# Splitting projections between small products, masking sooner, and forming bonus sums early in a hybrid decoder step

## The chip, the cores and the metric

The kernel runs on one core of a Trainium2 chip, as one launch of one program. The time is the device time of that launch in microseconds (us); less is better.

## The reference

One inference step of one layer, for 256 new prompt rows and 8 sample sequences of 8 rows (320 rows of 1024 together, all float32).

```
h = rmsnorm(x); proj = h @ w_in                       # 3840 columns
# HGRN2 group (4 heads of 128): chunked gated linear recurrence with states
# RWKV-7 group (8 heads of 64): r, k, v and low-rank decay, a, g from proj, mixed with the row before
kk = k * k_k / |k * k_k|;  k = k * (1 + (a - 1) * k_a)
S_t = S * w + (S . -kk) (kk * a)^T + v k^T;  y = S_t . r       # per token and head, state 64 x 64
bonus = sum_over_a_head(r * k * r_k) * v
y = (groupnorm(y) + bonus) * g
x = x + concat(o_hgrn, y) @ w_out
x = x + moe(rmsnorm(x))                                # top 4 of 32 experts, clamped SwiGLU
return rmsnorm(x), both groups' new states, last normalised rows
```

## The kernel before

Everything is written by hand: each engine has its own list of instructions in the order in which it issues them, and semaphores order the engines against each other. The work around the change is the mixer of the layer, before the experts.

**Projections.** `w_in` is read in 15 chunks of 256 columns into a ring of three slots (`WORDER`, `NSLOT`). SyncE's list loads chunk n when the tiles of chunk n - 3 are done. Each chunk gives two tiles, so there are 30 projections, numbered 0 to 29; `proj_part(n, c0, c1)` issues the matmuls c0 to c1 of the eight 128-row steps of tile n. ScalarE evicts each tile into `raw`, and VectorE mixes it with the row before (`mix_tile`) or gates it (`gate_tile`), in the order of the tile numbers.

**PSUM.** Each product that fills a bank is a unit. `psum_units()` names, in the order of TensorE's list, the units with their bank (the third argument of `add`), and in a second list (`ends`, `end(...)`) the order in which they are completed. `free(stage, i)` on TensorE waits until the unit that had the bank before has been read (`<stage>_ready`); `wait_filled` on a reader waits for the count of completed units. A unit whose bank is another one waits for another reader.

**The RWKV part.** The token-by-token recurrence is solved in chunks of 64 tokens. Gram products of the scaled rows (`gM`, `gN`, `gT`, `gK`, `gRb`, `gRk`; 64-row matmuls, L1126 and L1136) feed a triangular solve by doubling in five steps (`make_z`, `make_w`, `make_t`, L1152 and L1160; `take_z`, `take_w`, `take_t` on VectorE). Between the steps TensorE's list has projections 23 to 29 (L914). `W_` and `T_` start from unit matrices, which GpSimd copies into `hx` (L823) when the scaled rows are ready (`rw_ready`). The hidden states of the HGRN2 group are made by `hstate` (L1014) and added on VectorE (L2623, L2624).

**The sample sequences.** Their states are turned (`s0t`), multiplied with queries (`Rs`, L1254 and L1272), and give `Us` (L1283) and the values `Ys` (L1318 to L1320). `state_update(jj)` (L1214) makes the new HGRN2 states in two halves from itoks masked by sequence (`masked(jj)` on ScalarE, 8 copies); VectorE adds them (`add_states`, L2713). `bks` (L1301) holds the turned, decayed keys of the samples; `btok` and `ktok` (`turn_tokens`, L1313) hold the turned keys of the prompt.

**The bonus.** VectorE makes r * k * r_k into `rbon` (L2603). Late in the part, after the products `UW` and `UX` (L1332), four matmuls with a block matrix of ones sum over each head and spread the sum over its 64 rows (L1339); VectorE multiplies by v (L2781). Then follow `C` (L1351) and the accumulation of the states (L1505, L1508).

**Weights.** `w_out` is loaded in two halves: `wo[1]` into the `spare` slot, after all chunks of `w_in`, and `wo[0]` when projection 27 is done. The expert weights start when the units `Y0` are complete.

## Time and profile before

| | |
|---|---|
| median of 3 runs | 1212.39 us (1211.2 to 1213.39) |
| the profiled execution | 1214.35 us |
| its span (first to last instruction) | 1212.4 us |
| busy share of the span | TensorE 98%, VectorE 36%, ScalarE 21%, GpSimd 4% |
| mean granted TensorE clock | 0.998 of full speed |
| HBM read | 430.01 MB |

The span runs from the first to the last instruction of the program; the execution's time has about 2 us more around it. A start in the profile is counted from the span's start. TensorE's matmuls are pipelined, so a busy share near all of the span doesn't say that it works at its peak. An idle time in brackets behind an instruction is that of its engine just before it, with what ended it; "issue" means that nothing in the profile ended it.

### The profile page before, as it was taken

What the parts mean: (1) busy time and instruction counts of PE and PEld (TensorE: products, weight loads), DVE (VectorE), ACT (ScalarE), POOL (GpSimd) and SP (SyncE); (2) the same over time, 40 slices, a digit from 0 to 9 for tenths busy, and PEclk for the clock granted to TensorE, in tenths of its full rate; (3) what the DMA queues carried; (4) which work ended last, traced back from release to release, by engine and by line L of the source; (5) the groups of instructions that cost most, each with busy time, mean ns of one, the idle gap of its engine ahead of it and who ended that gap; (6) DMA issues with size and microseconds to landing.
All of it is one profiled execution on the core that took longest, in us unless ns stands there. A gap on an engine that the chain in (4) does not pass through costs nothing.

```text
span 1212.4 us, 18239 instructions
## 1 busy us (share of the span) xinstructions
PE 1187.4 (98%) x7814; PEld 572.9 (47%) x7814; DVE 440.9 (36%) x962; ACT 259.5 (21%) x630; POOL 44.7 (4%) x101
## 2 busy tenths in 40 slices
PE   8999999999999999999999999999999999999996
PEld 6777677745344344444443444344444444343332
DVE  3357954753413332332233132313322323232324
ACT  3114435422221111111121212021111111111213
POOL 8000110100000000000000000000000000000000
PEclk9999999999999999999999999999999999999999
DMA  9732302498999999999999999999999999999996
GB/s 285 183 105 71 122 31 72 125 414 334 409 426 429 426 414 428 426 432 431 431 429 431 431 431 432 431 426 431 429 432 432 430 430 431 432 432 428 422 424 231
DMA packets 49387, 436.09 MB, mean 360 GB/s; under 512 B 11525, under 2 KB 26952, under 8 KB 31770
## 3 DMA queue, kind: packets, MB, share of 16 engines
q1 hardware_dynamic: 48180, 431.74, 86.4%
q0 software_dynamic: 960, 3.02, 0.8%
q8 instruction: 63, 1.03, 0.3%
q10 hardware_dynamic: 166, 0.15, 0.0%
q14 instruction: 18, 0.15, 0.0%
HBM read 430.01 MB, written 4.89 MB: 359 GB/s over the span
## 4 chain that ended last, share of the span: by engine, by line
PE 86%; DMA 10%; DVE 2%; issue 1%; SPq 0%; ACT 0%; DVEq 0%
PE bank L1634 33%; PE bank L1670 16%; PE bank L914 9%; PE bank L1600 7%; DMA ring<-in_w_gate_up 5%; PE bank L1704 4%; PE bank L1395 3%; DMA ring<-in_w_down 3%; PE bank L1661 3%; DMA mix<-in_w_gate_up 2%; PE bank L1695 1%; PE bank L1152 1%; PE bank L901 1%; PE bank L947 1%; DMA hx<-in_state_shift 0%
## 5 line engine op out<-in xcount | busy, mean ns | idle before, releaser
L1634 PE MATMUL bank<-ring,mix 128*64 128x512 f32 x1504 | 344.8, 598 | 3.3 <-DMA ring<-in_w_gate_up 3.1
L1634 PEld LDWEIGHTS bank<-ring,mix 128*64 128x64 f32 x1504 | 101.3, 136 | 201.0 <-issue 197.7
L1670 PE MATMUL bank<-ring,mix 128*64 128x512 f32 x736 | 168.2, 598 | 0.8 <-DMA ring<-in_w_down 0.8
L2986 DVE TENSOR_TENSOR hTb<-bank,w2a 128x512 f32<-128x512 f32 x32 | 22.1, 692 | 361.3 <-PE bank L1661 361.3
L914 PE MATMUL bank<-hTb,ring 128*128 128x328 f32 (+1 forms) x416 | 120.6, 444 | 0.0
L2218 ACT ACTIVATE mix<-bank,nf 128x256 f32<-128x256 f32 x64 | 26.8, 470 | 431.3 <-PE bank L1600 431.2
L1634 PE MATMUL bank<-mix 128*64 128x512 f32 x500 | 112.7, 595 | 1.8 <-DMA mix<-in_w_gate_up 1.8
L3046 DVE TENSOR_TENSOR mix<-mix,bank 128x512 f32<-128x512 f32 x70 | 48.2, 688 | 159.5 <-PE bank L1704 143.5
L914 PEld LDWEIGHTS bank<-hTb,ring 128*128 128x128 f32 x416 | 77.8, 192 | 33.8 <-issue 2.0
L1670 PEld LDWEIGHTS bank<-ring,mix 128*64 128x64 f32 x736 | 49.3, 136 | 89.9 <-issue 84.0
L1634 PEld LDWEIGHTS bank<-mix 128*64 128x64 f32 x500 | 35.1, 137 | 71.7 <-issue 70.0
L1600 PE MATMUL bank<-mix,hx 128*128 128x256 f32 x240 | 66.1, 418 | 0.0
L3014 DVE SCALAR_TENSOR_TENSOR y_low<-bank,gc,y_high 64x512 fp32r<-64x512 f32 x62 | 46.5, 750 | 49.6 <-ACT y_high L2293 49.1
L1600 PEld LDWEIGHTS bank<-mix,hx 128*128 128x128 f32 x240 | 55.5, 300 | 9.1 <-issue 8.4
L2293 ACT ACTIVATE y_high<-bank,gc 64x512 fp32r<-64x512 f32 x62 | 42.3, 682 | 74.1 <-DVE gc L3028 38.3
L2273 ACT COPY g2w<-bank 128x512 f32<-128x512 f32 x64 | 34.3, 593 | 99.8 <-PE bank L1634 99.8
L1670 PE MATMUL bank<-mix 128*64 128x512 f32 x240 | 54.8, 598 | 0.0
L1704 PEld LDWEIGHTS bank<-y_high,slot_rows 128*128 128x128 f32 (+1 forms) x96 | 16.2, 186 | 62.5 <-issue 62.5
L1661 PEld LDWEIGHTS bank<-idg,g2w 128*128 128x128 f32 x256 | 33.2, 209 | 26.0 <-issue 26.0
L2283 ACT ACTIVATE bank<-hTb 128x512 f32<-128x512 f32 x32 | 19.2, 602 | 113.9 <-DVE hTb L2988 113.9
L1704 PE MATMUL bank<-y_high,slot_rows 128*128 128x512 f32 (+1 forms) x96 | 42.3, 480 | 0.0
L1661 PE MATMUL bank<-idg,g2w 128*128 128x128 f32 x256 | 39.3, 296 | 0.0
(448 smaller groups left out, 1086.7 us busy)
## 6 DMA issues: line engine op xcount, KB each, us to landing
ring<-in_w_gate_up SPq DMA_DIRECT2D x30, 4096.0 KB, 22.9
ring<-in_w_gate_up SPq DMA_DIRECT2D x33, 2048.0 KB, 14.4
ring<-in_w_down SPq DMA_DIRECT2D x15, 4096.0 KB, 23.7
mix<-in_w_gate_up SPq DMA_DIRECT2D x10, 4096.0 KB, 23.7
ring<-in_w_down SPq DMA_DIRECT2D x14, 2048.0 KB, 13.8
mix<-in_w_gate_up SPq DMA_DIRECT2D x11, 2048.0 KB, 13.2
mix<-in_w_down SPq DMA_DIRECT2D x5, 4096.0 KB, 25.0
ring<-in_w_in SPq DMA_DIRECT2D x14, 1024.0 KB, 5.5
```

The costliest lines, as they stand in the source:

```text
L914: last_ = mm(b_[:, 0:nn], slot(chunk)[:, c, P * k:P * k + P], hT[:, c, 0:nn], start=(c == 0), stop=(c == KT - 1))
L1395: last_ = mm(o_, lhs_, wo[c_ // 4][:, c_ % 4, 512 * h_:512 * h_ + 512], start=(c_ == 0), stop=(c_ == KT - 1))
L1600: last_ = mm(o, rows_of(tile_, c, r), sel[tile_][0:TN[tile_], :], start=(first and tile_ == TORD[0]), stop=(tile_ == TORD[2]), skip_group_ ...
L1634: last_ = mm(b_[64 * half:64 * half + 64, :].rearrange("s (p q) -> s p q", q=4), toks, cols[:, half], start=(c == 0), stop=(c == KT - 1))
L1661: last_ = nc.tensor.transpose(b_[:, P * q:P * q + P], src[:, q:NCOL:4], ident[:, :])
L1670: last_ = mm(b_[r:r + 64, :], lhs, w[:, o:o + NCOL], start=(j == 0 and q == 0), stop=(j == 1 and q == 3))
L1704: last_ = mm(o[:, :], scatr[r[g], g, P * tile_:P * tile_ + P], y_[r[g], g, :], start=(y_ is yhir and g == half), stop=(stop and y_ is ylor ...
L2218: ins = a(xg[n // 4 % 2][:, 256 * c:256 * c + 256], b[:, 256 * x:256 * x + 256], ACT.Copy, scale=nf2[int(n // 4 >= EW // 4)][:, c:c + 1])
L2273: cp(o, b[:, :]).then_inc(S("gu_read"), 1)
L2293: ins = a(yhir[r, k, :], banks[2][r, :], ACT.Copy, scale=gc[r, g:g + 1])
L3014: ins = v.scalar_tensor_tensor(out=ylor[r, k, :], in0=banks[2][r, :], scalar=gc[r, g:g + 1], in1=yhif[r, k, :], op0=ALU.mult, op1=ALU.subt ...
L3046: ins = v.tensor_tensor(o, o, b[:, :], ALU.add)
```

## The change

1. The bonus sums are formed early, in a new unit `bsum` behind `hosa`: four matmuls of 32 columns each put a head sum into rows of one bank, and ScalarE copies it into `rbon[:, 0, :]`. Where the bonus matmuls stood, each of the four tiles now has two matmuls that are 32 rows deep and spread one row of `rbon` over 64 rows. VectorE's bonus products wait for all four.
2. The unit matrices are copied into `hx` by ScalarE, behind the eviction of projection 22, instead of by GpSimd.
3. The load of `wo[1]` moves from behind the last chunk of `w_in` to a place ahead of chunk 6.
4. Projections are divided anew: 25 as 4 + 2 steps, W(1), 2 steps; 28 as 5 steps, W(3), 3 steps; 29 as 4 steps, then Z(4), `Us` and `gRk`, then 4 steps. The completion order and the banks follow.
5. `masked(1)` on ScalarE moves ahead of the copy of `Us`; `bks` moves ahead of `R0` on TensorE and on ScalarE; on VectorE the gating of projection 29 moves behind `gRk`.
6. The `Ys` products come all before the turned keys, and grouped by kind, the two row halves in turn; before, a quarter of them came ahead of each turned tile.

```diff
+    add("bsum", 1, (0,))
     add("hs2", 1, (1,))
     add("proj", 1, (7,))
-    add("gM", 3, (2, 3, 1))
+    add("gM", 3, (2, 3, 0))
     add("gN", 3, (4, 5, 6))
-    add("gT", 2, (7, 0))
-    add("s0t", 4, (5, 6, 7, 0))
-    add("gT", 1, (1,))
+    add("gT", 2, (7, 1))
+    add("s0t", 4, (5, 6, 7, 1))
+    add("gT", 1, (0,))
...
+    add("W", 3, (0, 1, 2))
     end("proj", 25)
-    add("W", 3, (0, 1, 2))
-    add("T", 3, (3, 4, 5))
-    add("gK", 3, (6, 7, 0))
+    add("T", 3, (3, 5, 6))
+    add("gK", 3, (7, 0, 4))
...
-    add("proj", 1, (3,))
+    add("proj", 1, (3,), ended=False)
     add("W", 2, (4, 5))
+    end("proj", 28)
...
-    add("proj", 1, (6,))
+    add("proj", 1, (7,), ended=False)
     add("Z", 2, (4, 5))
     add("Us", 1, (1,))
     add("gRk", 3, (2, 3, 4))
+    end("proj", 29)
     add("atok", 2, (5, 6))
+    add("bks", 1, (1,))
     add("R0", 2, (7, 0))
-    add("bks", 1, (1,))
...
@@ SyncE
+                if n == 6:
+                    load(wo[1], w_out[:, 4:8, :], "x1_wo1_in")
                 if n:
                     load(slot(n), w_in[:, :, 512 * g + 256 * u:512 * g + 256 * u + 256], f"ring{n % NSLOT}")
...
-            load(wo[1], w_out[:, 4:8, :], "x1_wo1_in")
@@ GpSimd
-            pool.wait_ge(S("rw_ready"), 1)
-            g.tensor_copy(hx[:, 0:2 * W5].rearrange("p (x t) -> p x t", t=64), mC[:, 6:7, :].broadcast_to([P, 2 * W5 // 64, 64]))\
-                .then_inc(S("eye_ready"), 1)
@@ TensorE
             filled(last, "hosa")
+            pe.wait_ge(S("rbon_in"), 4)
+            b = free("bsum", 0)
+            for j in range(4):
+                last = mm(b[32 * j:32 * j + 32, 0:NT], blk[:, 0:P:4], rbon[:, j, :], start=True, stop=True)
+            filled(last, "bsum")
             hstate("hs2", 1)
...
             make_z(1)
-            proj_part(25, 4, KT)
+            proj_part(25, 4, 6)
             make_w(1)
+            proj_part(25, 6, KT)
             make_t(1)
...
-            proj_part(28, 0, KT)
+            proj_part(28, 0, 5)
             make_w(3)
+            proj_part(28, 5, KT)
             make_t(3)
...
-            proj_part(29, 0, KT)
+            proj_part(29, 0, 4)
             make_z(4)
...
             gram("gRk", rk, rr)
+            proj_part(29, 4, KT)
             tokens("atok", rkk, 2)
...
             for j in range(4):
                 for p in range(2):
-                    o = b[half(p), half(j)]
-                    mm(o, us[half(p), j, :], Rb_[2][half(p), j, :], start=True, stop=False, skip_group_check=True)
-                    mm(o, vtoks[half(p), j, :], Rk_[2][half(p), j, :], start=False, stop=False, skip_group_check=True)
-                    last = mm(o, yts[half(p), j, :], ident[half(p), half(p)], start=False, stop=True, skip_group_check=True)
-                if j == 3:
-                    filled(last, "Ys")
+                    mm(b[half(p), half(j)], us[half(p), j, :], Rb_[2][half(p), j, :], start=True, stop=False, skip_group_check=True)
+                for p in range(2):
+                    mm(b[half(p), half(j)], vtoks[half(p), j, :], Rk_[2][half(p), j, :], start=False, stop=False, skip_group_check=True)
+                for p in range(2):
+                    last = mm(b[half(p), half(j)], yts[half(p), j, :], ident[half(p), half(p)], start=False, stop=True,
+                              skip_group_check=True)
+            filled(last, "Ys")
+            for j in range(4):
                 turn_tokens(("btok", "ktok")[j // 2], (ra, rk)[j // 2], j % 2)
...
-            pe.wait_ge(S("rbon_in"), 4)
+            pe.wait_ge(S("bonus_ready"), 1)
             for j in range(4):
+                r = slice(32 * j, 32 * j + 32)
                 b = free("bonus", j)
-                filled(mm(b[:, 0:NT], blk[:, :], rbon[:, j, :], start=True, stop=True), "bonus")
+                for p in range(2):
+                    c = 32 * j + 16 * p
+                    last = mm(b[half(p), 0:NT], ident[r, c:c + 1].broadcast_to([32, 64]), rbon[r, 0, :], start=True, stop=True)
+                filled(last, "bonus")
@@ ScalarE
                     a(hsq, htok, ACT.Square).then_inc(S("osq"), 1)
+                    ready(cp(rbon[:, 0, :], wait_filled("bsum", 0)[:, 0:NT]), "bonus")
+                if n == 22:
+                    act.wait_ge(S("rw_ready"), 1)
+                    a(hx[:, 0:2 * W5].rearrange("p (x t) -> p x t", t=64), mC[:, 6:7, :].broadcast_to([P, 2 * W5 // 64, 64]), ACT.Copy)\
+                        .then_inc(S("eye_ready"), 1)
...
                         ready(own_rows(e, rRs, 0), "Rs")
-                if n == 29:
+                    masked(1)
                     ready(cp(us[:, :, :], wait_filled("Us", 0)[:, 0:256].rearrange("p (j v) -> p j v", v=RN)), "Us")
-            masked(1)
...
@@ VectorE
             take_z(4)
-            gate_tile(29)
             dve.wait_ge(S("unit_filled"), U("gRk", 3))
...
             set_masked("gRk", Rk_, 9, 11)
+            gate_tile(29)
...
             dve.wait_ge(S("gpre_ready"), 4)
+            dve.wait_ge(S("unit_filled"), U("bonus", 4))
             for j in range(4):
                 b = wait_filled("bonus", j)
```

## Rows read from the trace of the kernel before

**Rows 1.** The page: its span, instruction packets, and the chain by engine.

```profile
span 1212.4 us, 18239 instructions
...
q8 instruction: 63, 1.03, 0.3%
...
PE 86%; DMA 10%; DVE 2%; issue 1%; SPq 0%; ACT 0%; DVEq 0%
```

**Rows 2.** Waits of SyncE's queue: us in total, times, longest.

```profile
SPq L640 <- PE bank L1540: 47.4, 1, 47.4
```

**Rows 3.** TensorE's timeline, 119 to 227 us: start, duration, instruction, idle before.

```profile
119.85 0.77 PE L1008 MATMUL bank<-hx,g2w 128*32 128x320 f32 x8
...
145.75 0.62 PE L1136 MATMUL bank<-mix 64*64 64x64 f32 x13 [1.68 <-DVE ring L2624]
...
148.96 2.02 PE L1105 MATMUL bank<-idg,ring 128*128 128x128 f32 x16 [0.22 <-DVE hx L2655]
...
153.10 0.99 PE L1152 MATMUL bank<-hx,mix 64*64 64x64 f32 x53 [1.40 <-issue]
...
168.41 1.14 PE L1152 MATMUL bank<-mix,hx 64*64 64x32 f32 x64
...
172.39 1.09 PE L1126 MATMUL bank<-mix 64*64 64x64 f32 x59 [0.85 <-issue]
...
197.46 1.14 PE L1152 MATMUL bank<-mix,hx 64*64 64x32 f32 x64
...
200.90 0.42 PE L1272 MATMUL bank<-ring 64*32 64x64 f32 x23 [1.12 <-issue]
201.25 1.14 PE L1214 MATMUL bank<-ring 32*128 32x512 f32 x8
...
213.13 1.14 PE L1214 MATMUL bank<-ring 32*128 32x512 f32 x8
...
222.79 2.42 PE L1339 MATMUL bank<-mix,g2w 128*128 128x320 f32 x8
...
226.12 0.30 PE L1505 MATMUL bank<-ring,hTb 64*64 64x64 f32 x8
```

**Rows 4.** TensorE between its pauses: length, busy (matmuls), clock, DMA share, GB/s.

```profile
153.09:172.38 19.29, 18.43 (x507) 1.00 0.04 13
172.38:200.89 28.51, 27.39 (x760) 1.00 0.22 77
```

**Rows 5.** GpSimd's timeline at the copy of the unit matrices.

```profile
141.12 2.52 POOL L823 COPY hx<-mC 128x2560 f32<-128x2560 f32 x1 [34.67 <-DVE dc L2617]
```

**Rows 6.** All runs of VectorE's L2481: ns least, median, most; first and last start.

```profile
L2481 DVE TENSOR_TENSOR hx<-raw x14: 174/174/2106, 69.8 to 169.6; 128x8 f32<-128x8 f32 x14
```

**Rows 7.** ScalarE's timeline, its longest operation before the change's place.

```profile
137.97 1.27 ACT L2100 ACTIVATE ring<-mix 128x1280 f32<-128x1280 f32 x1
```

**Rows 8.** DMA issues: count, KB each, us from issue to landing.

```profile
spare_slot<-in_w_out SPq DMA_DIRECT2D x1, 2048.0 KB, 11.7
```

**Rows 9.** VectorE's timeline, 170 to 227 us.

```profile
170.37 0.95 DVE L2689 TENSOR_TENSOR hx<-hx,bank 128x256 f32<-128x256 f32 x3
...
198.83 0.75 DVE L2689 TENSOR_TENSOR hx<-hx,bank 128x256 f32<-128x256 f32 x2
...
202.48 2.48 DVE L2713 TENSOR_TENSOR ring<-ring,bank 128x512 f32<-128x512 f32 x4 [1.52 <-PE bank L1214]
...
214.36 2.48 DVE L2713 TENSOR_TENSOR ring<-ring,bank 128x512 f32<-128x512 f32 x4 [0.78 <-PE bank L1214]
...
222.15 0.69 DVE L2775 COPY ring<-bank 64x512 f32<-64x512 f32 x1 [0.40 <-PE bank L1332]
...
224.90 1.68 DVE L2781 TENSOR_TENSOR mix<-mix,bank 128x320 f32<-128x320 f32 x4
```

**Rows 10.** DMA queues, from 150.6 to 153.1 us and from 194.9 to 197 us.

```profile
q8 instruction: 1, 0.02, 2.3%
...
q8 instruction: 1, 0.02, 3.1%
```

More of the change, by code:

```diff
@@ L174, in psum_units @@
     add("gRk", 3, (2, 3, 4))
+    end("proj", 29)
     add("atok", 2, (5, 6))
+    add("bks", 1, (1,))
     add("R0", 2, (7, 0))
-    add("bks", 1, (1,))
     add("hsend", 4, (2, 3, 4, 5))
     add("W", 2, (6, 7))
-    add("Ys", 1, (0,), ended=False)
+    add("Ys", 1, (0,))
     add("btok", 2, (1, 2))
-    add("ktok", 2, (3, 4), ended=False)
-    end("ktok", 0)
-    end("Ys", 0)
-    end("ktok", 1)
+    add("ktok", 2, (3, 4))
     for x in range(2):
@@ L604, in _ @@
                 params(nm, A[src].rearrange("a (h p) -> (a h) p", p=P))
+            w_out = A["w_out"][0].rearrange("(c p) n -> p c n", p=P)
             for n, (g, u) in enumerate(WORDER):
@@ L632, in _ @@
                              A["norm_ffn"][0].rearrange("(j p r) -> p j r", p=P, r=r), "router_in")
-            w_out = A["w_out"][0].rearrange("(c p) n -> p c n", p=P)
-            load(wo[1], w_out[:, 4:8, :], "x1_wo1_in")
             sync.wait_ge(S("unit_filled"), U("proj", 28))
@@ L863, in free @@
                     s, k, _ = UNITS[BEFORE[n_]]
-                    s, k = {"nmT": ("params", 1), "bc": ("params", 2), "params": ("params", 3), "hT": (("hT", "hTo_lb")[k % 2], k // 2), "S0": ("S", k + 2), "Y0": ("Y", k), "xo": ("xo", k + 1)}.get(s, (s, k))
+                    s, k = {"nmT": ("params", 1), "bc": ("params", 2), "params": ("params", 3), "hT": (("hT", "hTo_lb")[k % 2], k // 2), "S0": ("S", k + 2), "Y0": ("Y", k), "xo": ("xo", k + 1), "bonus": ("bonus", k + 1), "bsum": ("bonus", 0)}.get(s, (s, k))
                     pe.wait_ge(S(f"{s}_ready"), k + 1)
@@ L1285, in _ @@
             gram("gRk", rk, rr)
+            proj_part(29, 4, KT)
             tokens("atok", rkk, 2)
+            pe.wait_ge(S("bk_scaled"), 2)
+            b = free("bks", 0)
+            for s, src in enumerate((ra, rk)):
+                for j in range(4):
+                    for p in range(2):
+                        o = 256 * s + 64 * j
+                        last = mm(b[half(p), o:o + 64], src[half(p), j, NP_:NT], ident[half(p), half(p)], start=True, stop=True)
+            filled(last, "bks")
             b = [free("R0", 0), free("R0", 1)]
@@ L1294, in _ @@
                             filled(last, "R0")
-            pe.wait_ge(S("bk_scaled"), 2)
-            b = free("bks", 0)
-            for s, src in enumerate((ra, rk)):
-                for j in range(4):
-                    for p in range(2):
-                        o = 256 * s + 64 * j
-                        last = mm(b[half(p), o:o + 64], src[half(p), j, NP_:NT], ident[half(p), half(p)], start=True, stop=True)
-            filled(last, "bks")
             state_update(1)
@@ L1316, in _ @@
                 for p in range(2):
-                    o = b[half(p), half(j)]
-                    mm(o, us[half(p), j, :], Rb_[2][half(p), j, :], start=True, stop=False, skip_group_check=True)
-                    mm(o, vtoks[half(p), j, :], Rk_[2][half(p), j, :], start=False, stop=False, skip_group_check=True)
-                    last = mm(o, yts[half(p), j, :], ident[half(p), half(p)], start=False, stop=True, skip_group_check=True)
-                if j == 3:
-                    filled(last, "Ys")
+                    mm(b[half(p), half(j)], us[half(p), j, :], Rb_[2][half(p), j, :], start=True, stop=False, skip_group_check=True)
[5 more added lines that the diff above has]
+            filled(last, "Ys")
+            for j in range(4):
                 turn_tokens(("btok", "ktok")[j // 2], (ra, rk)[j // 2], j % 2)
@@ L1335, in _ @@
                                 filled(last, ("UW", "UX")[p])
-            pe.wait_ge(S("rbon_in"), 4)
+            pe.wait_ge(S("bonus_ready"), 1)
             for j in range(4):
+                r = slice(32 * j, 32 * j + 32)
                 b = free("bonus", j)
-                filled(mm(b[:, 0:NT], blk[:, :], rbon[:, j, :], start=True, stop=True), "bonus")
+                for p in range(2):
+                    c = 32 * j + 16 * p
+                    last = mm(b[half(p), 0:NT], ident[r, c:c + 1].broadcast_to([32, 64]), rbon[r, 0, :], start=True, stop=True)
+                filled(last, "bonus")
             def head(x_, p_):
@@ L2142, in _ @@
                 ready(ins, "atok")
+            ready(cp(bks[:, :, :, :].rearrange("p s j v -> p (s j v)"), wait_filled("bks", 0)[:, :]), "bks")
             for p in range(2):
@@ L2149, in _ @@
                     ready(cp(o, b), "R0")
-            ready(cp(bks[:, :, :, :].rearrange("p s j v -> p (s j v)"), wait_filled("bks", 0)[:, :]), "bks")
             act.wait_ge(S("unit_filled"), U("hsend", 8))
@@ L2925, in _ @@
             sent(1)
-            dve.wait_ge(S("bonus_ready"), 4)
+            dve.wait_ge(S("bonus_ready"), 5)
             for j in range(4):
```

## The prediction

> **What bounds the kernel now.** I read the page first, then TensorE's timeline from 115 to 310 us, where every edit of this change lies, then for each of its pauses the timeline of the engine that it waited for. The page's chain of work gives TensorE 86% and DMA 10% of a span of 1212.4 us [rows 1]. The expert part, from about 236 us on, streams weights; its loads are released by SyncE after one wait of 47.4 us that TensorE's last state values end [rows 2]. So what the earlier part gains or loses up to that point moves the whole rest by as much. Nothing after it is edited but a counter value.
>
> Up to there TensorE is hardly ever idle, and its pauses are of two kinds. Two are named: 1.68 us at 145.75 and 0.22 at 148.96, both for VectorE [rows 3]. The others say "issue": 1.40 at 153.10, 0.85 at 172.39, 1.12 at 200.90 [rows 3]. They are not spread at will. From one to the next lie 507 and 760 matmuls [rows 4], four and six times 126.7. The page lists 63 instruction packets for 1.03 MB [rows 1], about 16 KB each. I read this as TensorE's program arriving in pieces of some 127 matmuls with their weight loads, and a pause where a piece is late. The pauses lie among 64-row products, which use up a piece in about 2 us; a projection of 4.5 us lets the next piece catch up.
>
> The first named pause has its cause on another engine. GpSimd's copy of unit matrices runs from 141.12 for 2.52 us [rows 5]; of the 14 subtractions of 8 columns on VectorE the median is 0.174 us, and one takes 2.106 [rows 6]: the one that meets the copy; both end near 143.65. The hidden-state update that TensorE waits for stands behind it.
>
> **The change, part by part.** All sums are made against the profiled execution (1214.35 us, its span plus 1.9) and carried to the median of the three runs, 1212.39, unchanged.
>
> *A, up to projection 24.* The copy goes to ScalarE. Its price is not in the trace; 1280 elements take ScalarE 1.27 [rows 7], so 2560 take about 2.5 (bounds 2.5 as on GpSimd, twice that for a source read by broadcast; I take the nearest row). It starts when the same vector instruction releases it, so it ends where GpSimd's did, near 143.6. The blocked subtraction falls back to 0.17; the bank of the third Gram part also changes from the hidden state's to the sums', evicted by ScalarE near 139.6. Each alone would end most of the 1.68. The pause of 1.40 falls in a stretch where a 2 MB output-weight load and a prior ring load keep the DMA engines full; that load (11.7 us from issue to landing [rows 8]) moves to about 46 us, ahead on SyncE's queue of projection weights that are needed four projections, some 18 us, later. The bonus sums are added here: the key-norm sums of the same form take 0.77 [rows 3]. So A = -(1.68 + 0.22 + 1.40) + 0.77 = -2.5. Bounds: 0 if the piece that paused at 153.10 is late in another place, -3.0 if pipeline refill after each pause goes too.
>
> *B, projection 25 to the key Gram.* Two of its last four steps now follow the product W(1). The vector engine's list still has the mixing of projection 25 ahead of W's additions. Before, the additions began at 170.37, 1.96 after the projection's end at 168.41, and three of them took 0.95 [rows 3, 9]; the first is thus done 2.28 after that end. Now only T(1) lies between the end and the Gram (estimate 1.35: W and T fill some 2.7 of the 3.1 from 168.41 to where the pause before 172.39 begins), whose bank 0 needs that addition: a new wait of 2.28 - 1.35 = 0.9. What queues behind it on TensorE are the Gram and projection 26. It stands where the 0.85 "issue" pause was, and while TensorE waits the next piece can arrive. I take B = 0, bounds -0.85 and +0.9.
>
> *C, projection 28.* W(3) moves ahead of the last three of eight steps. Before, from the projection's end (197.46) the state update starts 3.79 later, at 201.25, with the 1.12 pause inside; the additions of W(3) that free its banks end at 198.83 + 0.75, 2.12 after that end [rows 3, 9]. Now W(3) (about 1.0; 1.14 in its row with the pipeline's tail) precedes that end, and the update follows it by 2.12 + 0.1: 0.6 gained, since T(3) and the products between take only some 1.5. Against it stands the next piece. Counted in steps of 127 matmuls from 172.39, one boundary lies near 191.35 and the next just inside W(3). The packet for it is listed only after 194.9 [rows 10], 3.6 us behind the boundary, while the other output-weight load fills the DMA engines; a piece is usable some 2.4 after its packet starts, as at 153.10 for the one listed after 150.6 [rows 10]. That is 197.35: just in time before, but W(3) now comes 1.65 sooner relative to the same load. I take a pause of 1.3. C = +0.7, bounds -0.6 and +1.0.
>
> *D, to the second state update.* The same matmuls in another order. Z(4) now follows four of eight steps of projection 29 and needs two banks that the state additions (2.48 us from 202.48 [rows 9]) free; they end 3.7 after the update's start where TensorE arrives at 3.3, and the projection itself waits 0.1 for T(3). D = +0.5, bounds 0 and +0.7. ScalarE's sooner masking (8 copies) and the moved copies have the rest of projection 29 as cover; uncovered they would cost 2.4.
>
> *E, the tail.* Here TensorE's work shrinks: Ys groups by kind instead of by position, and the spreading matmuls (two partition halves at a time, 32 rows deep; estimate 0.8 for all, like the equally many narrow ones of the sums) replace the 2.42 of the bonus [rows 3]. But TensorE is not what ends this stretch then. After the second update (213.13) VectorE starts its additions at 214.36 and reaches the bonus products at 224.90, idle in it only 0.40 for the products of W [rows 3, 9]. The accumulation at 226.12 needs the bank that the first bonus product (0.42) frees. So it can start 1.23 + 10.54 - 0.40 + 0.42 = 11.8, with a semaphore's step 11.85, after the update instead of 12.99. E = -1.1; bounds 0 and -1.1. The other 2 us that TensorE saves turn into waits.
>
> Sum: -2.53 + 0 + 0.7 + 0.5 - 1.14 = -2.5, so 1211.85 for the profiled execution and **1209.9 us** for the median.
>
> **Rivals.**
> *Pieces set the pace.* If pieces 127 matmuls apart always need about 4 us, a pause that is removed comes back at the next boundary among small products: about 1.2 in the Gram of A, 1.1 at T(0), 0.7 at the head turns. For it speak the exact spacing of the pauses and that the added sums move every later boundary by some 8 matmuls; against it the pieces that arrive in time behind each projection. A would be near 0.4 gained, the whole 0.3: 1212.1.
> *W(3) not held.* If the packet for it does not queue behind the load, C is -0.6 and the sum -3.8: 1208.6. Against it speaks the row at 194.9; for it, that the packet of one boundary is little to judge by. The Trainium skill, "DMA: Bandwidth & Descriptors", section "Queues, rings and completion order", has each engine take turns between queue rows packet by packet, by which an instruction packet would wait for one packet of the load and not for most of it; this trace does not agree at 191.35, where 3.6 us passed.
> *ScalarE's copy is slow (the other side).* ScalarE's copy of the next raw tile, and behind it VectorE's mixing and unit-matrix selection, queue behind it. About 1 us of slack is left, so from 3.5 us on every further us is lost; at 8.4 us (three and a half times the row's pace) it has eaten the 2.5 gained and 2.4 more: 1214.8 and above. For it speaks only that no broadcast source of this size runs on ScalarE before.
>
> **How the numbers follow.** About 0.2%, 2.4 us, is what a measurement of this kernel tells from no change: 1210.0 is the line to faster, 1214.8 to slower. The main case gets 0.52, with a range of its own of 1208.9 to 1210.9; the forecast lies at the line, so 0.29 of it counts as faster, 0.23 as same. W(3) not held 0.21, faster. Pieces set the pace 0.20, same. The slow copy, 0.07, slower. Together faster 0.50, same 0.43, slower 0.07. The range reaches from 1207.4 (W(3) not held, and B's pause gone without its new wait: 1.1 below 1208.6) to 1212.7 (pieces set the pace, D and C at their upper bounds).
>
> **What would show it.** In the changed profile: the 8-column subtraction at 0.17 every time, no pause for the hidden-state update, projection 24 starting 2.5 earlier; a wait near 0.9 before the key Gram, for VectorE; a pause just inside W(3) with its instruction packet late; TensorE waiting one to two us before the accumulation of state, for VectorE's bonus product. Wrong would make it: pauses of over 1 us at new places in A, a ScalarE copy well over 2.5, or an accumulation that starts later than 12 us after the second state update. The granted clock is full (1.00, the 2.4 GHz level) in all these stretches [rows 4], so no term hangs on it.

## The result, and the profile after

The changed kernel takes 1215.41 us in the median of 22 runs (1213.4 to 1218.67); before takes 1213.39 in as many beside it. The ratio is 1.0020, with a 95% interval from 1.0013 to 1.0028: slower by 2.0 us between the medians and by 1.6 to 3.4 by the interval, where 2.5 us of gain were forecast. The ratios in this document leave out one execution, of the run with 12 turns below, which took 3094.88 us.

The page of the changed kernel, its lines that answer to [rows 1]:

```profile
span 1213.6 us, 18274 instructions
...
q8 instruction: 64, 1.05, 0.4%
...
PE 87%; DMA 10%; DVE 2%; issue 1%; ACT 0%; SPq 0%; DVEq 0%
```

It has 35 more instructions and one more instruction packet. SyncE's one long wait, [rows 2], still ends with the last state values:

```profile
SPq L641 <- PE bank L1552: 47.1, 1, 47.1
```

TensorE's timeline, with the pauses (start, duration, instruction, idle before), answers to [rows 3]:

```profile
128.00 1.37 PE L912 MATMUL bank<-hTb,ring 128*128 128x328 f32 x4
...
147.75 2.02 PE L1108 MATMUL bank<-idg,ring 128*128 128x128 f32 x16 [0.21 <-DVE hx L2671]
...
151.54 1.16 PE L1155 MATMUL bank<-hx,mix 64*64 64x64 f32 x64 [1.19 <-issue]
...
153.10 4.68 PE L912 MATMUL bank<-hTb,ring 128*128 128x328 f32 x16
...
161.68 0.30 PE L1163 MATMUL bank<-hx,mix 64*64 64x32 f32 x2 [0.99 <-issue]
...
172.48 1.16 PE L1129 MATMUL bank<-mix 64*64 64x64 f32 x64 [0.93 <-DVE hx L2705]
...
197.03 1.02 PE L1155 MATMUL bank<-mix,hx 64*64 64x32 f32 x57 [0.76 <-issue]
...
202.05 1.14 PE L1217 MATMUL bank<-ring 32*128 32x512 f32 x8 [0.73 <-DVE hx L2705]
...
214.06 1.14 PE L1217 MATMUL bank<-ring 32*128 32x512 f32 x8
...
220.40 1.98 PE L1340 MATMUL bank<-ring,hx 64*64 64x128 f32 x64 [0.77 <-ACT hTb L2174]
...
224.56 1.16 PE L1363 MATMUL bank<-hTb,ring 64*64 64x64 f32 x64 [1.46 <-ACT ring L2181]
226.10 0.34 PE L1517 MATMUL bank<-ring,hTb 64*64 64x64 f32 x8 [0.38 <-DVE mix L2798]
...
238.09 0.50 PE L1388 MATMUL bank<-mix 64*64 64x64 f32 x9 [0.80 <-issue]
238.53 1.98 PE L1407 MATMUL bank<-ring,mix 128*128 128x512 f32 x4
```

T(n), W(n) and Z(n) are the products that `make_t`, `make_w` and `make_z` issue in step n. The first named pause, 1.68, is gone. Of the pauses marked "issue" the one of 1.40 is still there with 1.19, now at 151.54. New ones stand in T(0) (161.68), inside W(3) (197.03), and at 238.09, in the first values of the state chain, where before had none. The waits named for VectorE before the key Gram (0.93) and the state update (0.73), and for ScalarE before the products with W in the tail and before C (0.77, 1.46), are new as well. Of VectorE the 8-column subtraction, and of ScalarE the copy that came from GpSimd, answer to [rows 6] and [rows 5]:

```profile
L2497 DVE TENSOR_TENSOR hx<-raw x14: 174/175/176, 69.8 to 171.1; 128x8 f32<-128x8 f32 x14
```

```profile
141.08 2.34 ACT L2116 ACTIVATE hx<-mC 128x2560 f32<-128x2560 f32 x1 [1.20 <-DVE dc L2633]
```

**A common point.** Executions differ by up to 2.3 us ahead of the change: the first matmul of projection 1 starts at 14.2 us in one profile and at 16.5 in another, and the difference stays. So I measure stages from the first matmul of projection 22 (128.01 in before, 128.00 after), ahead of every edit but an early load. Both kernels were profiled a second time (last experiment). In us from that point:

| starts at | before | before, again | after | after, again |
|---|---|---|---|---|
| projection 24 | 26.53 | 26.55 | 25.10 | 25.37 |
| projection 25 | 34.07 | 34.08 | 33.91 | 34.18 |
| projection 26 | 45.93 | 45.82 | 46.04 | 46.31 |
| first state update | 73.24 | 73.14 | 74.05 | 74.59 |
| second state update | 85.12 | 84.71 | 86.06 | 86.60 |
| accumulation S0 | 98.11 | 96.94 | 98.10 | 98.63 |
| first output matmul | 109.66 | 108.21 | 110.53 | 111.35 |

The last line is the measure of a run below, "the stretch" (238.53 - 128.00 = 110.53). From that matmul to a late one of the expert part, the 1201st from the end, lie 690.73, 690.74, 690.73 and 690.72 us. So whatever the stretch gains or loses, the rest keeps. The change is 0.87 us slower in the first pair and 3.14 in the second; the medians' 2.0 lies between.

### The profile page after: what moved, and what is told of

Read it like the earlier page. It is cut to its first block, busy times and chain, and to the rows that moved or that the text cites. A ratio compares the mean times of both kernels' runs of the same rounds, so it can differ in the third digit from the quotient of the medians.

```text
span 1213.6 us, 18274 instructions
## 1 busy us (share of the span) xinstructions
PE 1185.9 (98%) x7830; PEld 571.1 (47%) x7830; DVE 439.1 (36%) x962; ACT 262.0 (22%) x632; POOL 42.2 (3%) x100
## 4 chain that ended last, share of the span: by engine, by line
PE 87%; DMA 10%; DVE 2%; issue 1%; ACT 0%; SPq 0%; DVEq 0%
PE bank L1646 33%; PE bank L1682 16%; PE bank L912 10%; PE bank L1612 8%; DMA ring<-in_w_gate_up 7%; PE bank L1716 4%; PE bank L1407 3%; DMA ring<-in_w_down 3%; PE bank L1673 3%; PE bank L1707 1%; PE bank L899 1%; PE bank L1155 1%; PE bank L945 1%; PE bank L1749 0%; PE bank L1129 0%
## 6 DMA issues: line engine op xcount, KB each, us to landing
ring<-in_w_down SPq DMA_DIRECT2D x14, 2048.0 KB, 14.2
```

## The experiments

**Theory.** TensorE's program comes in pieces, and by the spacing of the pauses [rows 4] a piece is 256 instructions, where a matmul and its weight load are two and a wait that stands by itself is one. Counted so from the start of each trace, the 52 pauses of 0.3 us and more that are marked "issue" between 115 and 245 us, in the 18 profiles of this document, all leave a remainder of 192 to 195 when divided by 256, wherever an edit moved them in the work. In the changed kernel too, two whole pieces lie between the pauses at 151.54 and 161.68 (window of that stretch: length, TensorE's busy time and matmuls first):

```profile
151.54:161.68 10.14, 9.14 (x255) 7.32 (x255) 4.88 (x13) 3.31 (x11) 2.06 (x13) 1.00 0.02 3
```

I call the end of a piece a cut. A cut in a stretch of small products costs a pause when its piece is late, and a piece is late for two reasons: the piece before was used up too fast (where no load is in the way, the pauses in these runs end 2.9 to 4.3 us behind the cut before), or a load held up its packet. The change moves all later cuts by 17 instructions from the sums on and 33 from the bonus on, and leaves loads where packets want to pass. **Rival:** the cuts cost what they cost before, and the new order loses through its own waits for VectorE and ScalarE.

### Cuts moved, nothing else

In the first run 17 matmuls of projections 19 to 21 get one more waiting instruction; in the others an 8x8 turn is repeated n times ahead of the first parameters.

```diff
+ if (n_ in (20, 21) and c) or (n_ == 19 and c > 4):
+     for s_, v_ in [('ident_ready', 1), ('nm_brow_in', 16)]:
+         pe.wait_ge(S(s_), v_)
```

```diff
+ for _ in range(12):   # the other run: 4
+     nc.tensor.transpose(bank("nmT", 0)[0:KT, 0:KT], ident[0:KT, 0:KT], ident[0:KT, 0:KT])
  pe.wait_ge(S("nm_brow_in"), 16)
```

> The kernel before, with 17 more waits in TensorE's program, one each in 17 matmuls of the projections 19 to 21, for a semaphore that was reached at the start: no work, no order and no bank is changed, only where the pieces of 256 instructions are cut behind them, by as much as the bonus sums shift it in the changed kernel. Theory of position (the changed kernel lost by where its pieces are cut): a new pause of about 1.0 us among T(0)'s products near 163.5, one of 0.6 to 0.8 behind the prompt's values near 240, the pauses at 172.39 and 200.90 stay or move by some matmuls; the first expert's weights are multiplied 1.5 to 3 us later than before, and the time rises by as much, to between 1.001 and 1.003. Rival (the new order of work and its waits for VectorE and ScalarE cost it): within 0.2 us of before, ratio 1.000.

> As the run with 12 turns, but with 4 of them: 16 instructions, the shift of the changed kernel within one, and without the 0.47 us that the 17 waits cost the run that shifted by waits. In that run the pauses summed to 4.4, against 4.1 in before, while its median was 1.8 us above before's. Theory of position, in its strong form (the shift alone explains the change's 0.2%): 1.001 to 1.002. In its weak form (17 instructions move pauses but add few): 1.000 within 0.0007, and what the change lost is lost with its own order.

> The kernel before, with 12 turns of an 8x8 piece of the unit matrix ahead of everything on TensorE, in a bank that is written over afterwards; each is four instructions, so the pieces behind are cut 48 instructions sooner in the work. They lie in the 2.35 us before the first parameters and the 1.62 us before the first tokens have landed, so they cost no time by themselves; projection 23 should start where it does in before. Theory of position: a cut at 147.03 moves some 0.5 us sooner, those in the small products fall closer together; from the distances of the cuts in before and 3.5 to 4 us for a piece I work out pauses that sum to 3 to 7 us more than before's 4.1, 1.003 to 1.006. Rival (only the work's own order and waits count): 1.000.

The expectations counted the turns wrongly. Their pages list 4 and 12 more matmuls, each with one weight load: the cuts moved by 8 and 24 instructions, not by 16 and 48. By instructions moved: 8 gives a stretch of 107.94 us and a ratio of 1.0010 (0.9999 to 1.0020); 17 gives 109.69 and 1.0015 (1.0005 to 1.0024); 24 gives 114.73 and 1.0029 (1.0017 to 1.0041). The run with 17 has a new pause of 0.44 in T(0), one of 0.49 in T(1) in place of the 0.85 just behind it, and 1.60 before the state update where before has 1.12; the pause of 0.6 to 0.8 that was expected behind the prompt's values is not there. In the run with 24 a pause of 1.69 at 201.69 is followed by half the clock. Its windows (length, busy and count of PE, PEld, DVE, ACT and POOL, granted clock, DMA share, GB/s):

```profile
197.00:201.00 4.00, 2.72 (x129) 2.02 (x127) 1.64 (x4) 0.75 (x2) 0.00 (x0) 1.00 0.03 6
201.00:206.00 5.00, 4.32 (x45) 2.18 (x46) 2.02 (x4) 2.06 (x8) 0.00 (x0) 0.53 0.01 3
```

So 24 instructions that do no work cost some 3.5 us (0.0029 of the median) by where they put the cuts. That the change's 17 alone explain its loss is not shown by this: 8 is not the change's shift, and its ratio lies at the lower end of the strong form while its stretch is shorter than those of before (108.21 and 109.66); at 17 the interval is wide.

The shift back in the changed kernel is a run that failed:

```diff
+ if 1 < n_ < 23 and c:
+     for s_, v_ in (("ident_ready", 1), ("nm_brow_in", 16), ("x0_wo0_in", 16)):
+         pe.wait_ge(S(s_), v_)
```

> The changed kernel, with 238 more waits of the same kind, two each in 119 matmuls of the projections 2 to 22: with the 17 of the bonus sums that makes 255, so from projection 23 up to the bonus the pieces are cut again where before had them, within one instruction. All of the change's work and order stays. Theory of position: no pause in T(0) near 161.7, none near 238 behind the prompt's values; the pause near 151.5 stays, since its piece is late for another reason; 1.5 to 2.5 us faster than the changed kernel, 0.999 to 1.000 of before. Rival: as slow as the changed kernel, 1.002, or slower by the waits' own 238 times 0.05 us where they are not hidden.

Three waits on a matmul that had none made one more instruction, not two: the page lists 18393, 119 more, so the cuts went to a third place. The pauses in T(0) and at 238 are gone as expected, but others came, each at a cut whose packet was wanted just after a load had started (142.68 and 191.63):

```profile
150.00 1.06 PE L1132 MATMUL bank<-mix 64*64 64x32 f32 x26 [3.84 <-issue]
...
198.98 0.35 PE L1261 MATMUL bank<-mix,ring 64*64 64x64 f32 x9 [3.68 <-issue]
```

The granted clock fell behind both (0.59 from 148 to 153, 0.71 from 198 to 203). The stretch is 120.25, the median 1226.01, the ratio 1.0113 (1.0095 to 1.0131). Shorter pauses of 1.03 at 216.92 and 1.45 at 241.32 stand at cuts too. Nothing follows for the shift that it was made for; it shows what badly placed cuts cost.

### Loads out of the packets' way

```diff
- sync.wait_ge(S("unit_filled"), U("proj", 2 * (n - NSLOT) + 2))
+ sync.wait_ge(S("unit_filled"), U("proj", 27 if n == 14 else 2 * (n - NSLOT) + 2))
...
- sync.wait_ge(S("unit_filled"), U("proj", 28))
+ sync.wait_ge(S("unit_filled"), U("hsend", 4))
  load(wo[0], w_out[:, 0:4, :], "x0_wo0_in")
```

> The changed kernel, with two loads issued later on SyncE's queue: the last 1 MB of projection weights after projection 26 (about 181 us, not 143.7) and the second 2 MB of output weights after the first state update (about 203, not 188.9). If the loads hold up the instruction packets (listed 3.5 us behind the cut at 145.69 and 3.3 behind the one at 191.34, against 0.6 to 1.5 at most others): packets near 147 and 193, the pauses of 1.19 at 151.54 and of 0.76 at 197.03 both gone, state update 0 up to 1.9 us sooner, 1.000 to 1.001 of before. Rival (the packet waits for TensorE's own program to reach some place, whatever the DMA engines do): both pauses stay and the ratio is that of the changed kernel, 1.002.

With the first of the two edits alone:

> The changed kernel, with only the last 1 MB of projection weights issued later (after projection 26), and the second output-weight load where the change has it. Splits what both gave together (3.4 us of the median). By the pauses: the one of 1.19 at 151.54 goes with this load, and the one of 0.55 in T(0) that went with it is shared; the one of 0.76 at 197.03 belongs to the output weights and stays. So 1.5 to 2.2 us faster than the changed kernel, 1.000 of before. If the output weights' load were what counts: 1.002 still.

And before with both, and with the change's early load of wo[1]:

> The kernel before with the three loads where the changed kernel with later loads has them (2 MB of output weights at about 46 us, the last 1 MB of projection weights after projection 26, the other 2 MB of output weights after the first state update), and all else as before. Packets held up by loads: the pause of 1.40 at 153.10 is gone, packets follow the cuts at 147.03 and 191.35 by 1.5 and less; 1.0 to 1.5 us faster, 0.999. If the rest of the change is worth nothing it is then level with the changed kernel with later loads (0.9987); if the change's order is worth the 2.5 that I summed, this one is 2 us above it.

The DMA queues of the changed kernel from the cut at 145.69 to where the packet starts, from there to the pause's end, and from the cut at 191.34 on (queue, packets, MB, share of the engines' time):

```profile
q1 hardware_dynamic: 954, 0.96, 84.9%
q0 software_dynamic: 62, 0.24, 18.1%
...
q8 instruction: 1, 0.02, 2.5%
...
q1 hardware_dynamic: 310, 1.27, 95.0%
```

The same for the version with both loads later, 144.3 to 145.3, and 145.3 to 146.5, where its packet starts 1.03 behind the cut at 144.28:

```profile
q0 software_dynamic: 67, 0.21, 73.6%
...
q8 instruction: 1, 0.02, 4.8%
```

Both packets come sooner (0.8 us behind the second cut, at 188.77), and both pauses are gone. Its timeline runs through where 1.19 stood, and keeps a shorter pause in T(0) and the wait for VectorE:

```profile
149.75 0.63 PE L1163 MATMUL bank<-hx,mix 64*64 64x64 f32 x16
150.31 4.68 PE L912 MATMUL bank<-hTb,ring 128*128 128x328 f32 x16
...
158.33 0.30 PE L1163 MATMUL bank<-hx,mix 64*64 64x32 f32 x2 [0.43 <-issue]
...
197.74 1.14 PE L1217 MATMUL bank<-ring 32*128 32x512 f32 x8 [0.73 <-DVE hx L2705]
```

| | stretch | median | ratio |
|---|---|---|---|
| change, ring load later | 109.38 | 1214.36 | 1.0016 (1.0007 to 1.0025) |
| change, both later | 107.26 | 1212.03 | 0.9987 (0.9978 to 0.9996) |
| before, three loads moved | 105.64 | 1210.24 | 0.9980 (0.9970 to 0.9990) |

With only the ring load moved the pause at 151.54 goes, but the one in W(3) is 1.03 instead of 0.76, with its packet 3.6 behind the cut under the other load. The median gives 1.1 against the changed kernel's first runs and 0.2 against its second, less than the 1.5 expected, and the intervals of the ratios overlap: what this load is worth alone is shown in the trace (1.4 us at projection 24) and not in the time. Both together are worth 3.4 us of the median, 4.0 by the ratios, and before gains 2.5 by its three; both are more than was expected. So the first theory holds for the two packets, against the rival by which they wait for TensorE's own program. That before with the same loads is faster still says that the rest of the change is a loss even where no load is in the way: some 1.6 us by these two profiles (107.26 - 105.64), 0.8 by the ratios, whose intervals overlap. By stage (changed less before, both with loads later): -1.20 up to projection 24, +0.72 to projection 25, +0.67 to 26, +1.13 to the first update, -0.08 to the second, -0.40 to S0, +0.78 behind it.

### The copy on ScalarE alone

```diff
- pool.wait_ge(S("rw_ready"), 1)
- g.tensor_copy(hx[:, 0:2 * W5]..., mC[:, 6:7, :]...).then_inc(S("eye_ready"), 1)
...
+ if n == 22:
+     act.wait_ge(S("rw_ready"), 1)
+     a(hx[:, 0:2 * W5]..., mC[:, 6:7, :]..., ACT.Copy).then_inc(S("eye_ready"), 1)
```

> The kernel before, with the unit-matrix copy on ScalarE instead of GpSimd and nothing else. The pause of 1.68 before the Gram's second half should go, and the 8-column subtraction fall from 2.1 to 0.17. Pieces set the pace: the cut before it then comes sooner, its packet too or not, and the pause at 153.10 grows; at most 0.4 us are left at projection 24, ratio 1.000. My prediction's own sum: 1.7 sooner at projection 24, and the same at the end, 0.9985. In the changed kernel 1.9 had been gained before the state turns, and 1.44 at projection 24, so I hold 1.0 to 1.6 for likeliest, 0.999.

> The kernel before with the three loads moved (0.998 so far) and the unit-matrix copy on ScalarE, nothing else of the change. The pause of 1.69 at 145.77 is the longest left there. With the loads out of the way the packet for the cut at 151.5 should follow the one before by 1 us, so the gain is kept: 1.3 to 1.7 us more, 0.9965 to 0.997. If pieces set the pace there even without loads, half of it comes back at the next cut: 0.9975.

Alone it brings 1.0001 (0.9991 to 1.0012). The 1.68 is gone, but the pause at the next cut has grown from 1.40 to 2.01, and projection 24 behind it runs at 0.76 of the clock and takes 6.36 where the changed kernel has 4.68 (timeline, then windows):

```profile
150.57 0.99 PE L1149 MATMUL bank<-hx,mix 64*64 64x64 f32 x53 [2.01 <-issue]
...
152.00 6.36 PE L911 MATMUL bank<-hTb,ring 128*128 128x328 f32 x16
```

```profile
148.50:153.00 4.50, 2.49 (x76) 2.15 (x74) 1.75 (x4) 1.61 (x3) 3.17 (x13) 0.89 0.87 352
153.00:158.00 5.00, 5.00 (x15) 3.11 (x14) 0.28 (x1) 0.00 (x0) 0.00 (x0) 0.76 0.01 3
```

With the loads moved the same copy keeps its gain: a stretch of 103.87, 1.77 less than without it, median 1208.23, ratio 0.9969 (0.9958 to 0.9980). That is a little more than the 1.3 to 1.7 expected.

### Without the splits, without the sums

Projections 25 and 28 whole again, then the sums left out, then both, all in the changed kernel with later loads:

```diff
- proj_part(25, 4, 6)
- make_w(1)
- proj_part(25, 6, KT)
+ proj_part(25, 4, KT)
+ make_w(1)
...
- proj_part(28, 0, 5)
- make_w(3)
- proj_part(28, 5, KT)
+ proj_part(28, 0, KT)
+ make_w(3)
```

```diff
- add("bsum", 1, (0,))
...
- pe.wait_ge(S("bonus_ready"), 1)
- for j in range(4): ...   # spreading, two halves each
+ pe.wait_ge(S("rbon_in"), 4)
+ for j in range(4):
+     b = free("bonus", j)
+     filled(mm(b[:, 0:NT], blk[:, :], rbon[:, j, :], start=True, stop=True), "bonus")
```

> The changed kernel with later loads, and with projections 25 and 28 whole again, each ahead of its product W. Between the changed kernel with later loads and the one before with the same loads, projection 25 to 26 differs by 0.67 (VectorE's additions of W(1) end later than the key Gram wants them) and projection 28 to the state update by 1.13. If these splits are the cost: both differences go, 1.5 us faster than the changed kernel with later loads, 0.9975 of before. If the cuts' place is, not the splits: 0.9987 still.

> The changed kernel with later loads, and without the early sums and their spreading: the bonus is formed at its old place by the old four matmuls. The 0.70 of the sums goes, and with their 17 instructions the pause in T(0) (0.43 in that profile) and part of the 0.53 behind the prompt's values; the bonus takes 2.4 again where the accumulation waited 1.46 for ScalarE's copy, so 0 to 0.4 is given back. 0.8 to 1.6 us faster than with the sums, 0.9975 to 0.998. If the sums paid for themselves, as my prediction has them do in its term for the tail (1.1): 0.5 slower, 0.999.

> The changed kernel with later loads, without the splits of projections 25 and 28 and without the sums: what is left of the change beside the loads is the copy on ScalarE, the new order from projection 29 to the turns, and ScalarE's sooner masking. Against the run with loads and copy alone (0.9969, 794.6 us from the common point to a late expert's matmul) it tells what the tail's order is worth. My prediction's terms D and E: 0.5 lost to the second state update, 1.1 gained behind it, so 0.6 faster, 0.9964. By the trace of the version without sums, VectorE's bonus product still ends that stretch 12.04 after the second update, 12.7 in the run with loads and copy, and D is 0.1 to 0.4 lost: 0.3 to 0.6 faster, not to be told apart in the medians. If splits and order only work together: slower than 0.9971.

| changed kernel with later loads | stretch | median | ratio |
|---|---|---|---|
| without splits | 105.99 | 1210.51 | 0.9981 (0.9972 to 0.9990) |
| without sums | 104.92 | 1208.92 | 0.9971 (0.9960 to 0.9982) |
| without both | 103.17 | 1208.07 | 0.9958 (0.9944 to 0.9971) |

Without splits projection 28 to the first update takes 6.88 instead of 8.02: the whole of the 1.13. Projection 25 to 26 gets only 0.30 of its 0.67, because a cut now falls in T(1) with a pause of 0.96. Without sums 2.34 us are gained, more than the 0.8 to 1.6 expected, where their own work is 0.70, and S0 starts 12.04 behind the second update as with them: VectorE sets that time, and the matmuls that the spreading saves save nothing. The version without both is the fastest run here. Its stretch is 0.70 shorter than that of the version with loads and copy alone, which the intervals don't separate. Its timeline at the first update, which no longer waits, and at the pauses left in the tail:

```profile
195.88 0.46 PE L1268 MATMUL bank<-ring 64*32 64x64 f32 x32
196.26 1.14 PE L1210 MATMUL bank<-ring 32*128 32x512 f32 x8
...
214.65 1.98 PE L1331 MATMUL bank<-ring,hx 64*64 64x128 f32 x64 [0.46 <-ACT hTb L2160]
```

### The sums' cuts without the sums

The version without sums, with 4 and with 8 turns ahead of everything. By the count above these are 8 and 16 instructions; 16 is the shift of the sums within one.

> The version without sums (0.9971; 795.7 us from the common point), with 4 turns of a piece of the unit matrix ahead of everything: the cuts up to the bonus stand where the sums put them, no work and no wait is changed. Theory of position: the pause in T(0) is back, 0.4 to 1.0 us, and projection 25 starts 0.7 to 1.2 later from the common point (30.54 without); 796.5 to 797.5 in all, 0.9978 to 0.9985. Rival (the sums' own waits): no pause in T(0), 795.7 and 0.9971.

> As the run with 4 turns, but with 8: 32 instructions, so that behind the bonus the cuts stand within one instruction where sums and spreading together put them. Theory of position: from the first state accumulation to the first expert output matmul 12.06 us, as in the changed kernel with later loads, and not 10.97 as without sums, with a pause of 0.5 in the values' chain; and a pause in T(0) too, so 797 to 798, 0.998 to 0.999. Rival: 10.97, and 0.9971.

With 8 instructions the stretch is 105.31 and the ratio 0.9973 (0.9963 to 0.9983): no pause in T(0), 0.11 at the start of projection 25. With 16 it is 108.24, 3.32 more than without, and 0.9992 (0.9983 to 1.0001), the median 2.3 us higher. T(0) runs through in the version without sums (first two rows); with 16 instructions in front it has the changed kernel's 0.99 again (second fence), and projection 25's first half runs at a lower clock behind it, 4.16 instead of 2.47 (third, a window):

```profile
156.65 0.64 PE L1157 MATMUL bank<-hx,mix 64*64 64x32 f32 x16
157.22 2.47 PE L911 MATMUL bank<-hTb,ring 128*128 128x328 f32 x8
```

```profile
158.00 0.24 PE L1159 MATMUL bank<-hx,mix 64*64 64x32 f32 x1 [0.99 <-issue]
158.16 4.16 PE L913 MATMUL bank<-hTb,ring 128*128 128x328 f32 x8
...
234.63 1.96 PE L1399 MATMUL bank<-ring,mix 128*128 128x512 f32 x4 [0.50 <-issue]
```

```profile
158.00:162.30 4.30, 4.30 (x13) 2.55 (x13) 2.38 (x5) 0.00 (x0) 0.00 (x0) 0.60 0.02 4
```

No sums, no spreading and none of their waits are in this version. So the pause in T(0) comes from the place of the cuts. From projection 24 to 25 the 16 instructions cost 1.22, where the change costs 1.27; 1.51 of the 3.32 come up to projection 26, by the lower clock, which the changed kernel does not have there. The size of a pause in T(0) goes with the time that its packet took to pass: 0.95 to 0.99 in the four profiles where that was some 1.4 us, 0.63 in the one with 1.1, and 0.43 or 0.44 in the three with 1.0. So part of the 3.32 may be that execution's. A pause of 0.50 near the first output matmuls appears too; from S0 to that matmul are 11.55, against 10.98 without the turns and 12.06 with the sums (33 instructions there), so the tail's share is shown in kind, not in full.

### Both kernels once more

> The kernel before once more, unchanged, for a second profile of it. In the profiles so far projection 1 starts anywhere from 14.2 to 16.5 us, a difference that stays to the end, so stretches have to be compared from a common point; projection 22's half (128.01 in before) serves. From there to the first expert's matmul (295.90) lie 167.9 us in before's profile, 168.8 in the changed kernel's, 163.9 to 166.6 in three of the others whose medians were not as much faster. If before's profile is a slow sample of this stretch, this one gives 166.0 to 167.0; if it is typical, 167.6 to 168.2. Ratio 1.000 either way.

> The changed kernel once more, unchanged, for a second profile. Its first one has 801.3 us from the common point to a late expert's matmul; before has 800.4 in one profile and 798.9 in another, and the medians are 2.1 to 2.4 apart. If the first profile is typical: 801 to 801.6, ratio 1.0015 to 1.002; if it was a fast sample, 802 and more.

Before, profiled again: a stretch of 108.21, 1.45 less than in its first profile, nearly all of it behind the first update, so the first was a slow sample; the ratio to itself is 1.0004 (0.9994 to 1.0014). The changed kernel again: 111.35 and 1.0014 (1.0004 to 1.0023); by the expectation's measure, now 802.1, its first was a fast sample. The pauses are those of the first profile, each at the same cut, two of them longer (1.46 at 152.18, 1.03 at 197.94), and one of 0.36 at 235.28 is new.

## Why the prediction was wrong

The forecast was carried to a median of 1212.39 from three runs; 22 runs give before 1213.39. So 1.0 of the 5.5 us between 1209.9 and 1215.41 is the base, and 4.5 is the change. Two steps failed: the sum prices the cuts where before has them, though the added instructions move them all, and it takes the 1.40 for gone, though only one of the two loads that it names for it moves and the other held the packet by itself. In the two pairs of profiles the sum is missed by 3.3 and 5.6 us: 1.1 and 1.35 in A, 1.3 and 1.3 in T(0), 0.9 and 1.45 behind S0, 0.1 and 1.55 in the other terms together.

**The transfer held.** "what the earlier part gains or loses up to that point moves the whole rest by as much": 690.72 to 690.74 us from the first output matmul on, in both kernels' four profiles. The error lies in the sum ahead of it. The pairs below are first profile against first, second against second.

**A** (forecast -2.5, measured -1.4 and -1.2) failed in one large term. The 1.68 went as read, with the subtraction back at 0.175 and ScalarE's copy at 2.34 for the 2.5 I took; the sums cost 0.70; the 0.22 stayed at 0.21. But the 1.40 was put down to "a 2 MB output-weight load and a prior ring load", and only the first of them moves. The ring load alone held the packet: 954 of its packets pass while the piece is awaited, the pause keeps 1.19 and 1.46, and with this load later it is gone. By the Trainium skill, "DMA: Bandwidth & Descriptors", section "Queues, rings and completion order", an engine drains a whole packet, typically some 9 to 17 descriptors and at most 64, from one queue row before it turns to the next. I had taken such a packet for one of those that the profile lists, and held from that that the skill and the trace differ; if each listed one is a descriptor, the 954 are some 60 for each of 16 engines, and the 310 behind the cut at 191.34 some 19, so the rows do not contradict the rule as it stands, though 60 is near its ceiling. Whether the packet or the request for it is held can't be seen in these traces.

**T(0)** is the step that was missing: +1.3 in both pairs, against a sum that has the cuts stay where they were. I had seen that "the added sums move every later boundary by some 8 matmuls", and priced T(0) at 1.1, but only in a rival. The turns without sums show that this is the cause.

**B** (0; +0.3 and +0.4): the wait of 0.93 before the key Gram is the 0.9 worked out. The 0.85 of "issue" that it was set against is gone from here as forecast; the one of 0.99 in T(0) stands one term earlier.

**C** (+0.7; +0.7 and +1.0) has the right size, by other parts. W(3) takes 2.02 and 2.30 with its pause and 1.06 without (both loads later), so the pause costs 0.96 and 1.24, not 1.3. Of the 0.6 of gain 0.27 came: the update follows the projection's end by 2.26 instead of 3.79, near the 2.2 forecast, but W(3) takes 1.06 of that and the divided projection 0.20 more. And the gain is owed to before's own pause of 1.12 on this way; where it is gone, before needs only 2.38 (before with loads moved):

```profile
195.47 1.14 PE L1153 MATMUL bank<-mix,hx 64*64 64x32 f32 x64
...
197.85 1.14 PE L1215 MATMUL bank<-ring 32*128 32x512 f32 x8
```

There the split pushes W(3)'s 1.1 ahead of that end and gets nothing for it; left out, it gives 1.13 back.

**D** (+0.5; +0.1 and +0.4) is right within its bounds.

**E** (-1.1; -0.95 and -0.2): the time itself was read well, 12.04 for the 11.85 forecast, with VectorE's bonus product at its end (`225.46 1.68 DVE L2798` in the changed kernel). What was mis-sized is the time it is compared with: 12.99 in the first profile of before holds a late piece of that execution, in W(4); the second has no pause there and needs 12.23. The first:

```profile
215.69 0.31 PE L1152 MATMUL bank<-mix,hx 64*64 64x32 f32 x5 [0.37 <-issue]
```

TensorE's saving turned into waits of 0.77 and 1.46 for ScalarE's copies more than into the one for VectorE (0.38).

**Behind S0** (0; +0.9 and +1.45): "Nothing after it is edited but a counter value" is true of the work and wrong of the time. The cuts there stand 33 instructions elsewhere, and a pause of 0.80 stands before the first output matmul in both profiles (238.09 and 239.29). The turns showed this one in kind, with 0.50.

**The rivals.** "Pieces set the pace" was right in kind and too small: 1.19 near the Gram of A where it had 1.2 (but by the ring load: with that later, and in before with loads and copy, no pause follows), 0.99 in T(0) for 1.1, nothing at the head turns for 0.7, and 0.80 behind the values that it did not have; it gave 1212.1. "W(3) not held" is refuted: the packet is listed 3.3 behind its cut under the load, and 0.8 without it. "ScalarE's copy is slow" did not happen. That the clock is full in these stretches, so that no term hangs on it, holds in both profiles of the changed kernel.

## What to carry to other kernels

Where TensorE runs small products, its pauses marked "issue" are a resource with places of its own: count instructions from one to the next, and treat every added or removed instruction as a shift of all later cuts, to be priced at each stretch that uses up a piece in less than some 4 us. See which load is in flight when each packet is due, and move that load before the work is reordered; here three loads were worth 2.5 us alone, and let a copy gain 1.8 that was worth nothing before. And profile the kernel before twice, since a step measured against one execution's pauses can be off by 0.8 us.

## What the runs showed of the hardware

A late piece can cost more than its pause. After a pause of 0.99 us among small products the granted clock was 0.60 over the next 4.3 us, and half a projection took 4.16 instead of 2.47; after 2.01 it was 0.76 over 5 us, and a projection took 6.36 for 4.68; after 1.69, 0.53, each a mean of the two levels, 1.2 and 2.4 GHz. After the same 0.99 in the changed kernel it stayed at 1.00:

```profile
161.68:166.00 4.32, 4.32 (x91) 3.27 (x92) 2.88 (x7) 0.00 (x0) 0.00 (x0) 1.00 0.02 4
```

What decides it these runs don't tell. In the profile of the copy alone (a stretch of 108.31, where before has 108.21 the second time) it took back what the copy gave: 1.68 saved, the next pause 0.61 longer, the projection behind it 1.68 slower.
